# Opening of a hybrid DiT block: early transposes of the normalised tokens, an earlier start for the modulation vectors, and the tap products moved inside the third convolution product

## The reference, cut to what matters

```python
mod_x = jax.nn.silu(c) @ w_ada + b_ada            # c: one vector of 2048
sh_x, sc_x, gt_x = jnp.split(mod_x, 3)
mod_c = jax.nn.silu(c_ctx) @ w_ada + b_ada
h_x = _rmsnorm(x, g_pre) * (1 + sc_x) + sh_x      # x: 512 tokens x 2048
h_c = _rmsnorm(ctx, g_pre) * (1 + sc_c) + sh_c    # ctx: 256 tokens x 2048
parts_x = _split_proj(h_x @ w_in)                 # xa, ba, ca, za, u, zb, f, zc, gates
u_c = h_c @ w_in[:, U_OFF:U_OFF + W_SSM]
# (A) short convolution: proj_a applied to ba * conv3(ca * xa) * silu(za)
# (B) diagonal state-space scan over u in both directions, then a GLU
# (C) Fourier mixing; three gated branches, one output projection, residual
```

## Time and profile before

| what | value |
|---|---|
| median of the runs | 2070.21 us |
| the profiled execution's own time | 2071.84 us |
| its span | 2070.1 us |
| PE busy in the span | 97% |
| ada, turns and first pieces | 17.8 us to 166.3 us |
| mean granted clock of the core | 0.994 |

### The profile page before, as it was taken

One profiled execution on the slowest core, in us unless ns is written; L12 is line 12 of the kernel. 1 busy time (PEld: TensorE's weight loads), 2 busy tenths in 40 slices (PEclk: granted clock), 3 DMA queues, 4 the chain that ended last, 5 costly groups with the idle time before them and its releaser, 6 DMA issues.

```text
span 2070.1 us, 26810 instructions
## 1 busy us (share of the span) xinstructions
PE 2011.0 (97%) x10085; PEld 1641.1 (79%) x10085; DVE 1088.7 (53%) x1641; ACT 587.6 (28%) x833; POOL 27.0 (1%) x16
## 2 busy tenths in 40 slices
PE   3999999999999999999999999999999999999998
PEld 0568888888888788888888888888788888888886
DVE  5445799888889645454334343433433333333325
ACT  3325333333333322222222222222322222221222
POOL 0003200000000000000000000000000000000000
PEclk9999999999999999999999999999999999999999
DMA  9873544434433544443334444443233333334423
GB/s 371 307 239 115 149 112 103 111 97 108 107 102 109 174 125 135 128 139 111 100 92 145 125 132 124 136 133 108 66 94 99 96 98 95 98 96 158 166 101 130
DMA packets 384079, 270.72 MB, mean 131 GB/s; under 512 B 24820, under 2 KB 349916, under 8 KB 382164
## 3 DMA queue, kind: packets, MB, share of 16 engines
q1 hardware_dynamic: 373664, 265.60, 41.6%
q10 hardware_dynamic: 10356, 4.35, 1.5%
HBM read 251.81 MB, written 18.09 MB: 130 GB/s over the span
## 4 chain that ended last, share of the span: by engine, by line
PE 80%; DVE 9%; DMA 4%; ACT 2%; issue 2%; ACTq 2%; SPq 0%; DVEq 0%
PE ac L716 21%; PE ac L717 21%; PE ac L720 21%; ACTq L1130 2%; DVE S L1606 2%; DMA M<-Tl 2%; PE ac L898 1%; PE ac L900 1%; PE ac L899 1%; DMA wslot<-w_in 1%; ACT S L934 1%; PE ss L900 1%; PE ss L898 1%; PE ss L899 1%; DVE wlo L1505 1%
## 5 line engine op out<-in xcount | busy, mean ns | idle before, releaser
L1505 DVE TENSOR_TENSOR wlo<-wslot,whi 128x1024 fp32r<-128x1024 f32 x309 | 378.3, 1225 | 643.1 <-ACT whi L934 639.0
L934 ACT ACTIVATE whi<-wslot 128x1024 fp32r<-128x1024 f32 x327 | 345.9, 1060 | 1244.8 <-PE ac L720 1028.6
L716 PE MATMUL ac<-hxh,whi 128*128 128x512 f32 x1664 | 651.9, 392 | 0.0
L717 PE MATMUL ac<-hxl,whi 128*128 128x512 f32 x1664 | 647.8, 389 | 0.0
L720 PE MATMUL ac<-hxh,wlo 128*128 128x512 f32 x1664 | 411.1, 389 | 0.9 <-DVE wlo L1505 0.9
L716 PEld LDWEIGHTS ac<-hxh,whi 128*128 128x128 f32 x1664 | 312.4, 188 | 67.6 <-issue 2.9
L720 PEld LDWEIGHTS ac<-hxh,wlo 128*128 128x128 f32 x1664 | 312.2, 188 | 66.1 <-DVE wlo L1505 1.3
L717 PEld LDWEIGHTS ac<-hxl,whi 128*128 128x128 f32 x1664 | 312.4, 188 | 63.8
L716 PE MATMUL ac<-bah,whi 128*128 128x512 f32 x384 | 149.4, 389 | 0.0
L717 PE MATMUL ac<-bal,whi 128*128 128x512 f32 x384 | 149.4, 389 | 0.0
L720 PE MATMUL ac<-bah,wlo 128*128 128x512 f32 x384 | 94.8, 389 | 0.0
(11 more groups left out here) (354 smaller groups left out, 2080.3 us busy)
## 6 DMA issues: line engine op xcount, KB each, us to landing
wslot<-w_in SPq DMA_DIRECT2D x224, 512.0 KB, 3.9
ring<-w_ada SPq DMA_DIRECT2D x64, 512.0 KB, 8.0
gwt<-w_ada SPq DMA_DIRECT2D x128, 128.0 KB, 2.5
wslot<-w_out SPq DMA_DIRECT2D x32, 512.0 KB, 3.5
wslot<-proj_a SPq DMA_DIRECT2D x16, 512.0 KB, 4.1
wslot<-proj_b SPq DMA_DIRECT2D x16, 512.0 KB, 4.1
wslot<-proj_c SPq DMA_DIRECT2D x16, 512.0 KB, 4.0
xn<-x SPq DMA_DIRECT2D x4, 1024.0 KB, 8.9
```

The costliest lines, as they stand in the source:

```text
L716: mm(ac[:, bank, :], w, xh, start=(v == 0 and q == 0), stop=False)
L717: mm(ac[:, bank, :], w, xl, start=False, stop=False)
L934: cp = lambda o, i, scale=1.0: nc.scalar.activation(o, i, ACT.Copy, scale=scale)
L1505: tt(wlo[:, s, :], wslot[:, s, :], whi[:, (U0[k] + j) % 2, :].bitcast(F32), ALU.subtract)\
```

## The change

- The two vectors `c` and `c_ctx` get a buffer of their own, are the first two transfers of SP (ahead of `x`), and are turned alone; sigmoid and `cs` take them out of PSUM. ACT's queue issues the three state-space transfers first, then `b_ada`, `g_pre`, `conv_w`, `ssm_d`. These are turned after `ada(3)` and copied in the middle of DVE's chain.
- Twelve of the sixteen token slices (`EARLY = 12`) are transposed before any scale is known: three after each of `ada(3)` to `ada(6)`, over the four `ac` banks; ACT copies each to `xT` in SBUF. `modulate` then reads `xT`. Only the last quarter keeps the old way.
- DVE: `token_scale` for the tokens moves behind the first part of the sine work. The rest (`zoh`, `chunk_powers`) goes behind the first quarter's slices. ACT no longer waits for `zn_done` before the first weight unit.
- PE: the `ada` units of a quarter are spread over its `x_piece`s and `c_piece`s. SP's order of the weight units and the context follows that.
- Convolution turn: the taps stand inside the third product, between its two units. ACT copies them before it splits weight unit 7. DVE adds the diagonal before the scan.

The diff, cut to its core:

```diff
@@ SP
+        for n, src in enumerate((c[0:1, :], c_ctx.rearrange("(a n) -> a n", a=1))):
+            sp.dma_start(crow[n * KD:(n + 1) * KD, :], ...).then_inc(cv_in, 16)
         for t in range(TT):
             sp.dma_start(xn[:, t, :], x[0, t * 128:(t + 1) * 128, :]).then_inc(x_in[t], 16)
+        for n in range(32):
             ada_unit(n)
+            if n % 8 >= 6:
+                first_unit(n // 8 * 2 + n % 2)
+            if n in (8, 9):
+                sp.dma_start(cn[:, n - 8, :], ctx[...]).then_inc(c_in, 16)
@@ PE
+        def early_turn(k):
+            pe.wait_ge(y_done, TT)
+            if k >= 4:
+                pe.wait_ge(xp_done, k - 3)
+            for t in range(TT):
+                last = tr(ac[:, k % 4, t * 128:(t + 1) * 128], xn[:, t, k * 128:(k + 1) * 128], ident[:, :])
+            last.then_inc(xp_ps, 1)
         for n in range(8):
             ada(n)
+            if n == 3:
+                pe.wait_ge(vec_in, 64)
+                tr(ss[:, 1, 0:V_END], vrow[:, :], ...)
+                tr(ss[:, 1, 128:128 + G], drow[...], ...).then_inc(vec_ps, 1)
+            if 3 <= n < 7:
+                for k in range(3 * (n - 3), 3 * (n - 2)):
+                    early_turn(k)
         cols(0)
+        ada(8)
+        ada(9)
+        pe.wait_ge(xp_done, EARLY)
+        for r in range(4):
+            x_piece(0, r, range(4))
+            ada(10 + r)
+        turn(0, 4)
+        ada(14)
+        turn(0, 5)
         for q in range(3):
+            if q:
+                x_piece(q, 0, range(4))
+                ada(8 * q + 12)
+                x_piece(q, 1, range(4))
+                turn(q, 4)
+                ada(8 * q + 13)
+                x_piece(q, 2, range(4))
+                ada(8 * q + 14)
+                turn(q, 5)
+                x_piece(q, 3, range(4))
+            ada(8 * q + 15)
+            c_piece(q, 0)
             cols(q + 1)
+            if q == 2:
+                turn(3, 0)
+            for r in range(1, 4):
                 c_piece(q, r)
+                if q < 2:
+                    ada(8 * q + 15 + r)
+                else:
+                    turn(3, r)
+            if q < 2:
+                ada(8 * q + 19)
@@ PE, conv_turn
-            product(1, b, 4, 2, 2, xs_of)
-            (the taps, signalled by k_ps)
+            product(1, b, 4, 2, 2, xs_of, mid=taps)
             product(1, b, 6, 2, 3, xs_of)
@@ ACT
+        for k in range(EARLY):
+            act.wait_ge(xp_ps, k + 1)
+            cp(xT[:, k, :], ac[:, k % 4, :]).then_inc(xp_done, 1)
+            if k == 8:
+                hi_first(0)
+        hi_first(1)
         rows_cp(0)
-        act.wait_ge(zn_done, 1)
-        hi_first(0)
@@ DVE, the slices
+                x_ = xT[:, k, :] if k < EARLY else ss[:, 3, :]
+                ts_(o, x_, mod[:, 0, k, 0:1], mod[:, 1, k, 0:1], ALU.mult, ALU.add).then_inc(ht_done, 1)
@@ DVE, conv_turn: these stood behind lo(1, b, 7), now ahead of the scan
+            dve.wait_ge(t_cp, b + 1)
+            (dd += diagonal taps, twice)
+            tt(o, o, dd[:, :, :], ALU.add).then_inc(t_add, 1)
```

More of the change, by code:

```diff
@@ L780, in conv_turn, with taps @@
                 last.then_inc(s_ps, 1)
-            product(1, b, 4, 2, 2, xs_of)
[L782 to L791, removed]
+            def taps():
+                pe.wait_ge(s_cp, 2 * b + 2)
+                pe.wait_ge(cp_done, b + 1)
+                for n in range(4):
+                    for dq in range(4):
+                        d, g = dq // 2, 4 * (dq % 2) + n
+                        at0 = (L - 1) * H if d == 0 else 0
+                        cp0 = 0 if d == 0 else H
+                        last = mm(ss[32 * dq:32 * dq + H, 0, n * 128:(n + 1) * 128],
+                                  V[:, d, g, at0:at0 + H], Cp[:, d, g, cp0:cp0 + L * H], start=True, stop=True)
+                last.then_inc(k_ps, 1)
+            product(1, b, 4, 2, 2, xs_of, mid=taps)
             product(1, b, 6, 2, 3, xs_of)
@@ L934, in _ @@
         cp = lambda o, i, scale=1.0: nc.scalar.activation(o, i, ACT.Copy, scale=scale)
-        for rr, src in ((V_C, c[0:1, :]), (V_CC, c_ctx.rearrange("(a n) -> a n", a=1)), (V_BADA, b_ada[0:1, 0:2 * D]),
-                        (V_GPRE, g_pre[0:1, :]), (V_CONV, conv_w)):
+        for i, src in enumerate((lam_re, lam_im)):
+            act.dma_start(lam[:, i, :], src[0].rearrange("d g p -> (d g) p")).then_inc(ssm_in, 16)
+        act.dma_start(ldt[:, :], log_dt[0].rearrange("d (g a) -> (d g) a", a=1)).then_inc(ssm_in, 16)
+        for rr, src in ((V_BADA, b_ada[0:1, 0:2 * D]), (V_GPRE, g_pre[0:1, :]), (V_CONV, conv_w)):
             n = src.shape[0] * src.shape[1] // 128
@@ L940, in _ @@
            .then_inc(vec_in, 16)
[L941 to L945, removed]
+        act.wait_ge(cv_ps, 1)
+        a(small[:, 0:32], ss[:, 0, 0:32], ACT.Sigmoid).then_inc(sg_done, 1)
         toks = [xn[:, t, :] for t in range(TT)] + [cn[:, t, :] for t in range(CT)]
@@ L978, in _ @@
             cp(toks[t], toks[t], small[:, 52 + t:53 + t]).then_inc(y_done, 1)
[L979 to L984 removed]
+        for k in range(EARLY):
[4 more added lines that the diff above has]
+        hi_first(1)
+        rows_cp(0)
+        for n in range(4):
             high(0, n)
@@ L1271, in _ @@
         link = st.link
[L1272 to L1277, removed]
+        st.link(v.memset(ss[:, 2, :], 0.0))
+        dve.wait_ge(id_done, 1)
         halves = ident[:, :].rearrange("p (kk h c) -> p kk h c", kk=2, h=2)
@@ L1353, in _, with zoh @@
         z = lambda n: ZN[:, n, 0, :]
[L1354 to L1368, removed]
+        def zoh():
+            link(tt(z(0), a6, a5, ALU.mult))
+            link(tt(z(1), a6, a4, ALU.mult))
+            link(ts_(a0, z(0), 1.0, None, ALU.subtract))
+            link(tt(a1, lre, lre, ALU.mult))
+            link(tt(a2, lim, lim, ALU.mult))
+            link(tt(a1, a1, a2, ALU.add))
+            link(v.reciprocal(a1, a1))
+            link(tt(a2, a0, lre, ALU.mult))
+            link(tt(a3, z(1), lim, ALU.mult))
+            link(tt(a2, a2, a3, ALU.add))
+            link(tt(z(2), a2, a1, ALU.mult))
+            link(tt(a2, z(1), lre, ALU.mult))
+            link(tt(a3, a0, lim, ALU.mult))
+            link(tt(a2, a2, a3, ALU.subtract))
+            link(tt(z(3), a2, a1, ALU.mult))
         def square(re, im, s, t):
@@ L1375, in square, with chunk_powers @@
             link(ts_(im, im, 2.0, None, ALU.mult))
[L1376 to L1382, removed]
+        def chunk_powers():
+            for _ in range(3):
+                square(a5, a4, a0, a1)
+                link(tt(a6, a6, a6, ALU.mult))
+            cpy(z(4), a5)
+            cpy(z(5), a4)
+            link(cpy(z(6), a6))
+            cpy(ZN[:, :, 1, :], ZN[:, :, 0, :]).then_inc(zn_done, 1)
         mod = vmod
@@ L1425, in _ @@
         for q in range(4):
+            if q == 0:
+                lo_first(0)
             columns(q)
             modulate(q, 0)
+            low(q, 0)
             modulate(q, 1)
-            low(q, 0)
-            lo_first(2 * q)
+            low(q, 1)
+            if q:
+                lo_first(2 * q)
             modulate(q, 2)
-            low(q, 1)
+            low(q, 2)
             modulate(q, 3)
-            low(q, 2)
+            low(q, 3)
             lo_first(2 * q + 1)
-            low(q, 3)
             if q == 0:
                 token_scale(TT, CT, 2)
[L1439 to L1442, removed]
+                zoh()
+            for n in range(4, 6):
+                modulate(q, n)
+                low(q, n)
+            if q == 0:
+                chunk_powers()
         dve.wait_ge(h_done, 24)
@@ L1600, in conv_turn @@
             lo(1, b, 6)
+            dve.wait_ge(t_cp, b + 1)
+            for q in range(2):
+                o = dd[:, 4 * q:4 * q + 4, :]
+                last = tt(o, o, ss[32 * q:32 * q + H, 0, :].rearrange("p (g c) -> p g c", g=4)[:, :, 0:H], ALU.add)
+            link(last)
+            o = Tl[:, :, 112:128]
+            tt(o, o, dd[:, :, :], ALU.add).then_inc(t_add, 1)
             for ri in range(2):
```

75 lines of the change are left out of this document (29 added, 46 removed).

## The result

The changed kernel takes 2057.24 us (median of 4 runs, 2055.88 to 2059.34), the kernel before beside it on the same chip 2070.63 (2070.14 to 2071.52). The ratio is 0.9934, with a 95% interval of 0.9919 to 0.9948: 13 us faster. The forecast was 2052.1: the gain came out 5 us smaller than forecast, inside the range.

A forecast was written before the change was run, and what follows sets the result against it. PE, busy nearly all of the span, was taken to bound the kernel, so its waits show where time can be won. Opening -10.4 and taps -7.7 sum to -18.1, giving 2052.1 us, range 2048.5 to 2060.5.

The forecast's parts named there:

- The constants: Opening: DVE's constants chain starts at 11 us, bounds 8.4 and 16.7, as lam and ldt now lead ACT's queue.
- The early turns: PE in the opening: starting at 34.4, three turns and one ada low, nine and three high; ada(7) ends at 46.9.
- Rivals 1: Opening: the clock stays low through the early turns; price +7.5, time 2059.6; chance 0.17.
- 2 (constants no earlier): Opening: the constants land no earlier (16.7); price +5.7, time 2057.8; chance 0.10.
- From there to the first x_piece: Opening, from ada(7)'s end at 46.9 through weight split, copies, cols(0), modulate and hand-overs: first x_piece at 52.0, -8.2.
- Behind it: Opening after the first x_piece starts: twelve turns of four transposes become four, -4.2; new waits +2.0.
- New waits: Opening behind the first x_piece: cols(1) waits 0.5, ring waits, last c_pieces hold weight unit 7; +2.0, bounds 0 and +6.
- The taps: Convolution turns: earlier taps let M's transfers leave 2.1 us earlier, removing PE's wait for M; -7.7, bounds 0 and -7.7.
- Rival 4: Convolution turns: the taps' wait only changes its name; price +7.7, time 2059.8; chance 0.06.
- Rival 3: Opening: the ring of w_ada units comes late all along; +4.5 at half of 22 units, 2056.6; chance 0.13.
- Rival 5: Opening: short waits keep PE at 1.2 GHz beyond the early turns; slower past 36 us, to 100 us 2076; chance 0.04.
- Opening: Whole opening: -8.2 up to the first x_piece, -4.2 behind it, +2.0 new waits, summing to -10.4.

The follow-up runs named there:

- the opening alone: Changed kernel with the convolution turn put back (taps behind the third product, diagonal behind low half 7): 2067.71 us, ratio 0.9982 to the kernel before.
- the context later: Changed kernel with each half of the context one w_ada unit later in SP's order: 2056.92 us, ratio 0.9931 to the kernel before.

## Why the prediction was right, and where it missed

- **The constants.** Forecast 11, bounds 8.4 to 16.7; measured 7.95, a little under the lower bound. Everything up to the scaled tokens moved with it: 31.3 for 34.4, the same 23.4 us of work behind. The run with the old queue order (18.78) shows that the place in the queue did it. The Trainium skill (DMA: Bandwidth & Descriptors, Queues, rings and completion order) has each engine take turns between queues by whole packets; the 8.4 that I drew from it was 0.5 off, but no run here singles out this way of sharing.
- **The early turns.** The step from the first turn to ada(7)'s end was forecast as 12.5 us and took 12.5 (31.36 to 43.8): clock low for three turns and one `ada`, then risen within the next three turns. Rivals 1 (clock low all along) and 2 (constants no earlier) are out.
- **From there to the first x_piece.** Forecast 5.1 us, measured 7.5. ada(9) waited 1.96 for its ring unit, which I had called "fit in between": 1 MB of context stands ahead of it on SP. The constants and with them the tokens were 3.1 us early against the forecast, this step 2.4 late; that the two nearly cancel, to -8.9 for -8.2, is luck.
- **Behind it: the step that failed.** "New waits ... I take +2.0, bounds 0 and +6." Measured +7.2, beyond the upper bound: 2.95 in ada(16), 2.9 in the last quarter (1.19 for a turn, and 2.12 for 0.41 at `wlo`), 1.3 for an x_piece at half the clock. The waits that the +2.0 was made of did not come: cols(1) runs without one, and so does every unit of the ring behind 52. The turns that went were worth 3.6, not 4.2 (0.45 each, since a c_piece with its turn takes 1.86 us and without 1.41). For ada(16) I looked at the wrong dependent. I took `chunk_powers` as hidden, and if not, x_piece(1,0) as late by a us or two. But columns(1) stands behind it on DVE, and the first `ada` of each next quarter, which on PE comes ahead of x_piece(1,0), may not overwrite the bank before columns has read it: `pe.wait_ge(col_rd, q)` in `ada`. And I did not follow DVE's new order modulate, low, modulate, low into the last quarter, where there is one PSUM bank for all four slices and no `xT`.
- **The taps.** Forecast -7.7, measured -8.2; `X` stays 2 us ahead. The transfers of `M` left 3.0 us earlier against unit 4, not 2.1. Rival 4 is out: the run with the taps alone has no new wait in its place. It came to 2062.28 for 2062.4 expected, in part by chance, since before was 1.05 slower beside it: a gain of 9.4 for 8.2.
- **Rival 3** (the ring late all along) did not come: behind 52 no ring wait is left in the changed kernel. **Rival 5** came in a small way: the clock did fall in the opening, for 7 us from 47.3 on, not for 36.

Opening -5.3 for -10.4, taps -8.2 for -7.7: -13.6 for -18.1. The mechanisms of both parts were right and the total stayed in its range, but the opening won half of what was forecast.

## What to carry to other kernels

Work that is "hidden" on another engine has two kinds of dependents: those that read its result, and those that read the result of what now stands behind it in that engine's queue; follow the second kind to the buffer that they free. When PE work moves to where data just arrives, its short waits can also cost by the clock: in these runs a wait of 2 to 3 us was sometimes followed by 3 to 7 us at half pace, and then cost 1.4 to 2.7 us more than its length. And if a chain starts with a small transfer, its place in its queue is the first thing to change.

## What the runs showed of the hardware

- The record of the granted clock reads 1.00 from the start of the program, while the matmuls run at the 1.2 GHz pace: in the changed kernel an `ada` takes 1.89 us at 34.11 and 1.04 at 37.92, with 1.00 on record at both. With the taps alone it reads 1.00 from 17 to 60 without a break, while every `ada` up to 41 takes 1.89. The record shows falls and the rise after one, not the first rise.
- Equal waits in equal places are followed by the low clock in one kernel's run and not in another's: 2.95 against 2.97 us at ada(16), 1.94 against 1.94 at `fT`, 2.12 against 2.13 at `wlo`. Where the clock fell at ada(16), the step to ada(20) took 11.4 to 12.7 us instead of 10.0, a price of 1.4 to 2.7; at `wlo` and at `fT` it was 1.6. The clock had not always held to the end of the wait: with the opening alone it fell at 78.4, and the wait ended at 79.48.
- 48 float32 transposes of 128x128 in a row went from about 0.23 to 0.12 us each, without any other matmul beside them (one execution).
- In the opening the clock stayed low for 6.8 us in the changed kernel, where PE waited 1.96 us in that stretch, and for 3.4 us with the context later, where it had no gap.
- A 128x1 transfer landed 6.2 us after its issue as third of its queue and 14.0 us as seventh, in both beside the 8 KB rows of `x` on SP's queue.
